# Second network: gate columns moved in beside the values' columns, in token layout, and the compression's first layer summed in four column groups

## The reference

```python
proj = x @ w_in[l]                      # 1024 x 2584 weights
(h_a, b_a, c_a, uv, q, kc, vc, ksl, vsl, kw, vw, gl) = jnp.split(proj, split_points, axis=-1)
y_a = short_conv(h_a, b_a, c_a, conv_w[l])
y_b = gmlp_spatial(uv, ...)
y_c = nsa_attention(q, kc, vc, ksl, vsl, kw, vw, gl, ...)
```

```python
def compress_kv(k, pe, w1, b1, w2):
    kb = k[:, idx]                      # blocks of 32 tokens x 64 features
    h = gelu(einsum("bnlgd,ldf->bngf", kb + pe, w1) + b1)   # sum over 2048 terms, 128 outputs
    return einsum("bngf,fe->bnge", h, w2)
```

## Time and profile before

| | us |
|---|---|
| median of 3 runs | 2038.51 (2038.29 to 2039.95) |
| profiled execution, its own time | 2038.37 |
| its span | 2036.4 |
| PE busy | 2013.8 (99%) |
| PE weight loads busy | 1835.1 (90%) |
| VectorE (DVE) busy | 1276.3 (63%) |
| ScalarE (ACT) busy | 927.4 (46%) |
| GpSimd (POOL) busy | 40.4 (2%) |
| granted clock, mean | 0.999 |

### The profile page before, as it was taken

One profiled execution on the slowest core, in us unless ns is written; L12 is line 12 of the kernel. 1 busy time (PEld: TensorE's weight loads), 2 busy tenths in 40 slices (PEclk: granted clock), 3 DMA queues, 4 the chain that ended last, 5 costly groups with the idle time before them and its releaser, 6 DMA issues.

```text
span 2036.4 us, 32522 instructions
## 1 busy us (share of the span) xinstructions
PE 2013.8 (99%) x14176; PEld 1835.1 (90%) x14176; DVE 1276.3 (63%) x1862; ACT 927.4 (46%) x1275; POOL 40.4 (2%) x56
## 2 busy tenths in 40 slices
PE   8999999999999999999999999999999999999998
PEld 7889999999787999999999989799999998979997
DVE  6566656555657665655665567765566556776555
ACT  4445544444445544544444454454444445444442
POOL 0000000000000000000000000000000000000000
PEclk9999999999999999999999999999999999999999
DMA  8544555665454455586566645458656664554663
GB/s 290 173 145 138 180 182 151 207 207 187 166 165 134 156 186 177 145 252 186 166 186 187 187 133 158 116 144 250 186 167 186 187 190 132 156 139 151 187 188 101
DMA packets 416134, 352.51 MB, mean 173 GB/s; under 512 B 28817, under 2 KB 361081, under 8 KB 415993
## 3 DMA queue, kind: packets, MB, share of 16 engines
q1 hardware_dynamic: 415992, 350.44, 56.9%
HBM read 349.36 MB, written 1.05 MB: 172 GB/s over the span
## 4 chain that ended last, share of the span: by engine, by line
PE 90%; DVE 6%; ACT 3%; issue 0%; DMA 0%; POOL 0%; SPq 0%; DVEq 0%
PE ps L201 28%; PE ps L202 27%; PE ps L203 27%; DVE hl L1978 2%; PE ps L1434 2%; ACT hl L1737 2%; PE ps L1515 1%; PE ps L1553 1%; PE ps L1587 1%; DVE er L2145 1%; DMA raw<-in_w_in 0%; DVE small L2104 0%; DVE xt L2055 0%; ACT tm L1779 0%; PE ps L1625 0%
## 5 line engine op out<-in xcount | busy, mean ns | idle before, releaser
L1978 DVE TENSOR_TENSOR hl<-raw,hl 128x1024 fp32r<-128x1024 f32 (+1 forms) x573 | 758.1, 1354 | 398.9 <-ACT hl L1737 397.4
L201 PE MATMUL ps<-xt,hl 128*128 128x256 f32 (+1 forms) x2672 | 753.9, 282 | 2.6 <-DVE hl L1978 2.6
L202 PE MATMUL ps<-xt,hl 128*128 128x256 f32 (+1 forms) x2672 | 746.0, 279 | 0.0
L203 PE MATMUL ps<-xt,hl 128*128 128x256 f32 (+1 forms) x2672 | 745.6, 279 | 0.0
L1737 ACT ACTIVATE hl<-raw 128x2048 fp32r<-128x2048 f32 (+1 forms) x323 | 612.9, 1899 | 187.0 <-PE ps L203 168.6
L201 PEld LDWEIGHTS ps<-xt,hl 128*128 128x128 f32 (+1 forms) x2672 | 500.9, 187 | 10.3 <-DVE hl L1978 4.0
L202 PEld LDWEIGHTS ps<-xt,hl 128*128 128x128 f32 (+1 forms) x2672 | 500.9, 187 | 3.2
L203 PEld LDWEIGHTS ps<-xt,hl 128*128 128x128 f32 (+1 forms) x2672 | 500.7, 187 | 0.2
L201 PE MATMUL ps<-hl,o 128*128 128x512 f32 x656 | 261.6, 399 | 0.0
L202 PE MATMUL ps<-hl,o 128*128 128x512 f32 x656 | 259.5, 396 | 0.0
L203 PE MATMUL ps<-hl,o 128*128 128x512 f32 x656 | 259.4, 395 | 0.0
(11 more groups left out here) (202 smaller groups left out, 1613.1 us busy)
## 6 DMA issues: line engine op xcount, KB each, us to landing
raw<-in_w_in SPq DMA_DIRECT2D x83, 1024.0 KB, 5.1
raw<-in_w_ffn_in SPq DMA_DIRECT2D x88, 512.0 KB, 5.2
raw<-in_ffn_gate SPq DMA_DIRECT2D x88, 512.0 KB, 4.0
raw<-in_ffn_up SPq DMA_DIRECT2D x88, 512.0 KB, 5.3
raw<-in_ffn_down SPq DMA_DIRECT2D x44, 1024.0 KB, 5.1
raw<-in_w_ffn_out SPq DMA_DIRECT2D x22, 1024.0 KB, 5.0
raw<-in_w_out SPq DMA_DIRECT2D x12, 1024.0 KB, 5.1
raw<-in_w_branch_a SPq DMA_DIRECT2D x8, 1024.0 KB, 5.0
```

Of the source, the lines that this page charges most:

```text
L201: e.matmul(out, l[0], r[0], start=start, stop=False)
L202: e.matmul(out, l[0], r[1], start=False, stop=False)
L203: return e.matmul(out, l[1], r[0], start=False, stop=stop)
L1978: e.tensor_tensor(lo[:, c], m["raw"][:, k % NRAW, 0:n][:, c], hi[:, c].bitcast(F), ALU.subtract).then_inc(s.low.up(("low", k), *([("low", ...
```

## The change

- The 24 gate columns lie behind the 256 value columns in the same weight units. There are two such units, of 4 row blocks x 280 columns (1120 per partition), instead of one of 2048 and one of 192. The tokens are stationary and the 280 columns move, so the gates come out with tokens on the partitions; each token half has a PSUM bank. The 24-row products and `gates_turn` with its transposes are gone. ScalarE takes the tanh from each bank, VectorE scales once.
- `lin_v` stands in the first mix in the place of `lin_gates`, and is gone from the second.
- `cmp_hidden` sums even and odd steps in separate column groups: 4 groups of 30 rows (start partitions 0, 32, 64, 96), 8 rounds of 4 matmuls. ScalarE copies all in one instruction. `cmp_gelu` is one matmul with a 0/1 matrix (`fold`, 60 columns, in the constants) that adds the two partial sums and turns them at once, in one bank in place of two. `compress` yields 1.0 after the first layer in place of 2.0.

```diff
@@ compress
-            yield 2.0
-            bs = [PB.take() for _ in range(2)]
+            yield 1.0
+            b = PB.take()
...
@@ lin_v
+            banks = [PB.take() for _ in range(2)]
+            for r in (0, 4):
+                w = w_in[r * 128:(r + 4) * 128, :].rearrange("(k p) c -> p k c", p=128)
+                segs = [(lambda a, c=c, n=n: a[:, 0:1120].rearrange("p (k c) -> p k c", k=4)[:, :, c:c + n], w[:, :, c0:c0 + n])
+                        for c, n, c0 in ((0, 128, 2176), (128, 128, 2432), (256, 24, 2560))]
+                g = P.unit(segs, 1120, True)
+                for i in range(2):
+                    add("kv_values", g, banks[i], i, r, xt_events(P.xv))
+                    P.spread(g, i + 1)
+                    if i == 0 or r == 0:
                         yield PART
+                P.spread(g, 3)
+            for i, b in enumerate(banks):
+                add("gates", l, b, gts[:, 24 * i:24 * i + 24])
+                add("copy", b, b.ap[:, 0:256], VS[:, i, 0:256], 1.0, before_q, [("v nsa", l, i)])
+                PB.give(b)
+            add("gates_scale", l, gts)
...
-        mix(chain(lin_cmp(), lin_k(), lin_gates(), lin_q(0)), early, 0.6, False)
+        mix(chain(lin_cmp(), lin_k(), lin_v(), lin_q(0)), early, 0.6, False)
...
-        mix(chain(lin_v(), lin_q(1), lin_conv(), beside(chain(lin_conv2(), lin_out()), conv)), steps, SHARE2)
+        mix(chain(lin_q(1), lin_conv(), beside(chain(lin_conv2(), lin_out()), conv)), steps, SHARE2)
@@ tensor_engine
-        for j in range(16):
-            for n in range(2):
-                ins = e.matmul(hb.ap[32 * n:32 * n + 30, 0:128], ka[:, 480 * n + j * 30:480 * n + (j + 1) * 30], w1[:, n, j * 128:(j + 1) * 128],
-                               start=j == 0, stop=j == 15)
+        for j in range(0, 16, 2):
+            for q in range(4):
+                n, x = q // 2, j + q % 2
+                ins = e.matmul(hb.ap[32 * q:32 * q + 30, 0:128], ka[:, 480 * n + x * 30:480 * n + (x + 1) * 30], w1[:, n, x * 128:(x + 1) * 128],
+                               start=j == 0, stop=j == 14, tile_position=(0, 32 * q))
...
+        e.matmul(b.ap[:, 0:60], tm.ap[0:126, 0:128], P.C("fold")[0:126, :], start=True, stop=True).then_inc(done.up(b.full, tm.free), 1)
...
+        for k in range(4):
+            ins = mm3(e, b.ap[:, 0:280], [XT[:, z, r + k, i * 128:(i + 1) * 128] for z in (0, 1)], [hi[:, k, :], lo[:, k, :]],
+                      r + k == 0, r + k == 7)
```

More of the change, by code:

```diff
@@ L72, in constants @@
     put("head", np.where((p[:, None] // 15) % 4 == np.arange(4)[None, :], 1.0, 0.0))
+    r = np.arange(60)
+    put("fold", np.where((p[:, None] // 64 == r[None, :] // 30) & (p[:, None] % 32 == r[None, :] % 30), 1.0, 0.0))
     return c
@@ L1112, in lin_cmp @@
             yield PART
[L1114 to L1126, removed]
         def lin_conv():
@@ L1646, in cmp_out, with kv_values @@
             done.up(vb.full, yr.free, ("w2 read", l)), 1)
-    def gates(l, g, b, tm, x_events):
-        hi, lo = (x.rearrange("p (k c) -> p k c", k=8) for x in hl(g, 192))
+    def kv_values(g, b, i, r, x_events):
+        hi, lo = (x.rearrange("p (k c) -> p k c", k=4) for x in hl(g, 1120))
         e.wait_ge(*T["low", g])
-        e.wait_ge(*T[b.before])
+        if r == 0:
+            e.wait_ge(*T[b.before])
         for x in x_events:
             e.wait_ge(*T[x])
[L1654 to L1674, removed]
+        for k in range(4):
+            ins = mm3(e, b.ap[:, 0:280], [XT[:, z, r + k, i * 128:(i + 1) * 128] for z in (0, 1)], [hi[:, k, :], lo[:, k, :]],
+                      r + k == 0, r + k == 7)
+        if r or i:
+            ins.then_inc(done.up(*([b.full] if r else []), *([("used", g)] if i else [])), 1)
     def gmlp_mix(l, i, b, zz, cols, cols_event):
@@ L1876, in cmp_hidden @@
         e.wait_ge(*T[tm.before])
-        for n in range(2):
-            ins = e.activation(tm.ap[32 * n:32 * n + 30, 0:128], hb.ap[32 * n:32 * n + 30, 0:128], ACT.Copy)
-        ins.then_inc(done.up(tm.full, hb.free), 1)
+        e.activation(tm.ap[0:126, 0:128], hb.ap[0:126, 0:128], ACT.Copy).then_inc(done.up(tm.full, hb.free), 1)
     def cmp_tanh(l, xyz, yr):
@@ L1887, in cmp_out, with gates @@
         e.activation(kcs, ob.ap[:, 0:15], ACT.Copy, scale=0.5).then_inc(done.up(("kcs", l), ob.free), 1)
-    def gates(l, g, b, tm, x_events):
+    def gates(l, b, gt):
         e.wait_ge(*T[b.full])
-        e.wait_ge(*T[tm.before])
-        e.activation(tm.ap[0:24, 0:256], b.ap[0:24, 0:256], ACT.Tanh, scale=0.5).then_inc(done.up(tm.full, b.free), 1)
+        e.activation(gt, b.ap[:, 256:280], ACT.Tanh, scale=0.5).then_inc(done.up(("gates tanh", l)), 1)
     def conv_split(l, yt, dst, before):
@@ L2235, in cmp_blocks, with cmp_gelu @@
         ins.then_inc(done.up(("ka", l), bank.free), 1)
[L2237 removed]
+    def cmp_gelu(l, b, tm, xyz, col, cols_event):
         x, y, z = xyz
[L2239 removed]
+        e.wait_ge(*T[b.full])
         e.wait_ge(*T[cols_event])
[L2241 to L2242 removed]
+        for n in range(2):
+            e.tensor_scalar(x[:, 30 * n:30 * n + 30], b.ap[:, 30 * n:30 * n + 30], col[:, n:n + 1], None, ALU.add).then_inc(done.up(b.free), 1)
         e.wait_ge(*done.now)
@@ L2264, in cmp_out, with gates_scale @@
                         bc(C("own")[0:120, :], 2, 64), ALU.mult).then_inc(done.up(("vb", l), vb.free), 1)
-    def gates_turn(l, b, tm, gts):
-        e.wait_ge(*T[b.full])
-        e.tensor_scalar(gts, b.ap[:, 0:48], 0.5, 0.5, ALU.mult, ALU.add).then_inc(done.up(("gates", l), b.free), 1)
+    def gates_scale(l, gts):
+        e.wait_ge(*T["gates tanh", l])
+        e.tensor_scalar(gts, gts, 0.5, 0.5, ALU.mult, ALU.add).then_inc(done.up(("gates", l)), 1)
     def conv_gate(l, bcg, hs):
```

34 lines of the change are left out of this document (8 added, 26 removed).

## The result

| | before | after |
|---|---|---|
| median of 7 runs | 2039.23 (2038.29 to 2039.95) | 2045.71 (2044.81 to 2046.17) |
| ratio, 95% interval | | 1.0031 (1.0022 to 1.0041) |
| span of the profiled execution | 2036.4 | 2042.9 |
| granted clock | 0.999 | 0.999 |

A forecast was written before the change was run, and what follows sets the result against it. PE was taken as the bound, busy 2013.8 of 2036.4 us. Work of -4.47 and waits of +0.5 gave -4.0 a layer, -8.0 for two, so 2030.5 us, range 2027.1 to 2035.0.

The forecast's parts named there:

- Step 6: Weight loading and splitting, the earlier start of the compression, and tanh and scaling on ScalarE and VectorE: no cost.
- A: Compression's first layer: four column groups are no faster than two, giving 2034.1 us; chance 0.14.
- D: Compression's first layer: the four groups run one after another, +2.9 in place of -1.81, giving 2039.9 us; chance 0.03.
- The forecast's own test: Wrong in kind if the first network or the feed-forward parts, where nothing is edited, move by more than 1 us.
- B: Attention: the new order's waits eat the gain, +3.8 us a layer, 2038.1; chance 0.10 at half to full price.
- C: From the values on, the weights run dry: 13 us a layer, giving 2056 us; chance 0.04.
- Step 1: Second network, each layer: the gates' 24 products go, -2.75 us.
- Steps 2 and 4: Each layer: 48 value products widen from 256 to 280 columns, +0.52 us; `gates_turn` goes, -0.43 us.
- Step 3: Compression's first layer: four column groups make 16 rounds in place of 32, -1.81 us a layer.
- Step 5: Attention waits, each layer: -0.34 at `values_t`, -0.83 then +0.7 at `cmp_turn`, +0.5 at `cmp_scores`, +0.5 elsewhere; sum +0.5 us.

The follow-up runs named there:

- e2_after_pad68: The changed kernel with 68 more unused columns in the constants tile, giving the operand distance of the kernel before: 2034.21 us, ratio 0.9974.
- e4_pad8: The kernel before with 8 unused columns in the constants tile, moving the tiles behind it up by 32 bytes: 2043.80 us, ratio 1.0025.
- e7_after_pad48: The changed kernel with 48 more unused columns in the constants tile, putting `xt` at distance 192 from `hl`: 2003.79 us, ratio 0.9826.

## Why the prediction was wrong, point by point

- **Step 6, "what I cost at nothing", is the step that failed**, and the sentence behind it, that the first network can't move since nothing there is edited. The diff had one more part, 60 columns in a tile that lies ahead of `xt`, and no step priced it. It cost 11.5 us, more than all steps together were to bring. The steps took the distance of two products, 0.115 us for 256 columns, as a property of the shape; it is one of the shape and of where the operands lie. No rival held this case: A to D are all local. The forecast's own test (a move of over 1 us in the first network means wrong in kind) is what showed it. Rivals B and C did not happen: the waits of this part grew by 0.8 us a layer, where those of B add up to 4.3, and no wait of `mm3` for a low part came in behind the values.
- **Step 1, the gates.** Right for the products themselves: in the kernel with before's layout the 24 are gone with their 2.75 us. The edited stretch as a whole is 2.61 us shorter where 4.0 were forecast; the points below say where the rest went.
- **Steps 2 and 4, the wider values and `gates_turn`.** +0.52 and -0.43 were forecast, +0.09 together. The 48 products of the values took 6.24 us before, with what stood among them, and 6.34 with 280 columns; the two transposes were 0.23 from start to next start. -0.13 together.
- **Step 3, four column groups.** -1.81 forecast, -1.73 measured. Rivals A and D fall. A pass now takes 1.89 / 64 = 29.5 ns, and a matmul of the program, two passes, 59. The figure of the Trainium skill that the prediction weighed (62 ns a matmul where microcode decodes it) is not a bound here. The same section of the Trainium skill names a floor of about 25 ns between starts. The mean of 29.5 is above it, but single starts are not: products in two column groups start within one hundredth of a microsecond of each other. No run here shows a floor between products in one group.
- **Step 5, the waits, mis-sized.** PE's idle time in the edited stretch, by the rows of stretches: 106.02 - 104.85 = 1.17 before, 103.41 - 101.42 = 1.99 with the edits in before's layout. +0.8 against +0.5 forecast. `values_t` behind `cmp_scores` lost its wait as said, `cmp_scores` waits 0.20 where 0.5 was forecast, and `cmp_turn` 0.83 where 0.7 was. But there was no row for what took their place: the transposes of the attention weights now wait 0.59 for ScalarE. The timeline of PE in `e2_after_pad68` there:

```profile
1292.16 0.62 PE L1428 MATMUL ps<-cst,er 128*128 128x128 f32 x4
1293.37 0.66 PE L1428 MATMUL ps<-cst,er 128*128 128x128 f32 x4 [0.59 <-ACT er L1808]
...
1295.36 0.39 PE L1672 MATMUL ps<-small,q 64*128 64x15 f32 x2
1295.95 1.06 PE L1672 MATMUL ps<-small,q 64*128 64x15 f32 x14 [0.20 <-DVE o L1966]
1296.94 0.50 PE L203 MATMUL ps<-hl,o 128*128 128x512 f32 x1
...
1303.31 1.00 PE L1509 MATMUL ps<-ai,xt 128*128 128x128 f32 x8
1305.14 0.33 PE L1679 MATMUL ps<-cst,er 128*120 128x128 f32 x1 [0.83 <-DVE er L2334]
1305.40 1.08 PE L1581 MATMUL ps<-et,v 128*64 128x256 f32 x8
```

That `cmp_turn` came so close to 0.7 is in part luck. The timeline of VectorE beside it:

```profile
1297.79 0.34 DVE L2313 TENSOR_TENSOR er<-ps,cst 128x60 f32<-128x60 f32 x2
...
1302.12 0.69 DVE L2091 COPY et<-ps 128x512 f32<-128x512 f32 x1 [0.60 <-PE ps L1428]
...
1303.86 0.27 DVE L2326 TENSOR_REDUCE small<-er 128x8 f32<-128x120 f32 x1
```

VectorE reached `cmp_scores` 0.85 us behind the scores (1297.79 against 1296.94), not 2.1. By the prediction's own sum no wait would be left. But its copy then waited 0.60 for the transposes on PE, and no term had that.

- **Work that was not in the sum.** Steps 1 to 4 measure -2.75 - 0.13 - 1.73 = -4.6 a layer. The stretch got 2.6 shorter and waits took 0.8; the other 1.2 us are busy time of products that are in both kernels, which lie between others in the new order. The starts in the two traces say where: the two `cmp_scores` take 0.40 more (one of them is stopped behind its second pass, and 1.38 without the wait stands where 1.07 stood), the two `cmp_turn` 0.40 (0.26 ahead of `values_t`, 0.08 ahead of `residual`), the transposes of the attention weights 0.30, products of 512 columns on `o1` 0.22; the four transposes of `sg` take 0.31 less. So a product's cost depends on its neighbour and on stops in its run, and the sum had none of that. Why the neighbours matter is not shown, and no run isolates it.
- **The sum.** Edits: -8.0 forecast, -5.4 and -5.8 measured in two layouts. With them alone the time would have been 2034.2 against 2030.5, inside the range, though a third of the gain was not there; PE's busy time fell by 6.9 us (2013.8 to 2006.9) where about 8 were forecast. The layout's +11.5 put it on the other side.

## What to carry to other kernels

Treat the size of any tile as part of a change: a few added columns move every tile behind them, and with them the pace of products that nobody touched. When PE is the bound, compare the distance from one product's start to the next in a part that was not edited before believing a sum over the edited one, and try an experiment that only pads. Then use the pad on purpose: a sweep of 8 distances between the stationary and the moving operand, here worth 30 us of 2034, is cheaper than most edits, but measure it in the whole kernel, since at some distances there are two paces and the products ahead can decide which.

## What was not expected of the hardware

- Products of the rounded 32-bit format start 113.3 to 120 ns apart for 256 moving columns and 227 to 234 for 512, at a granted clock of 1.0, by the distance of the two operands' addresses modulo 256 bytes; 106.7 and 213.3 would be the columns alone at 2.4 GHz. The Trainium skill, "SBUF — State Buffer", section "SBUF: two separate sides", says that within the engines' side only the port pair of VectorE and GpSimd is contended and TensorE never waits on anyone. The programs of products alone agree that no other engine is needed for this; they show that TensorE's own two operands are not independent of each other. What inside the chip does it, no run here shows.
- At distance 192 narrow products have two paces, 113.3 and 117.8 ns, and a series keeps the one it fell into; the same 96 instructions took 11.31 or 10.91 us. Both paces were also read once each for one pair at distance 64 (113.4 and 117.8).
- The best distance differs by width: 0 gives the fastest wide products and, with 96, the slowest narrow ones.
- The sign of the distance counts. Some products of 256 columns move `hl` over `xt` instead. In `e4_pad8` half of them start 114 ns apart or less, where those that move `xt` have a median of 118; in `e7_after_pad48` it is 118 against 113. That fits the table if its distance is read as moving less stationary operand.
